# A hybrid decoder layer on one core: first blocks and half the old states loaded before the mixing stage, U built first, two slices of the output weights split inside the second pass

## What is computed

```python
p = h @ w_in                                   # projection, h = rmsnorm(x)
qkv = silu(causal_conv(p[..., :QKV_DIM], ...))
# chunked gated delta rule: T = inverse of a 64x64 unit triangular matrix per head
u = einsum('bnhij,bnjhd->bnhid', T, v_beta)
w = einsum('bnhij,bnjhd->bnhid', T, k_beta * exp(gc)[..., None])
def step(S, inp):
    v_new = u_n - einsum('bhid,bhde->bhie', w_n, S)
    o = einsum('bihd,bhde->bhie', q_n, S) * exp(g_n) + einsum('bhij,bhje->bhie', qk_n, v_new)
    S = S * exp(g_last) + einsum('bihd,bhie->bhde', k_dec, v_new)
# sample rows: one recurrent step on state_delta (8 requests x 4 heads, 128x128 each)
kv = einsum('bhd,bhde->bhe', k_t, S);  delta = (v_t - kv) * b_t
y = concatenate([o_a, o_b]) @ w_o              # o_b is the chunk gMLP
```

## Time and profile before

| | |
|---|---|
| median of 3 runs | 2351.67 us (2350.78 to 2353.48) |
| the profiled execution | 2351.88 us, its span 2350.2 us |
| TensorE busy | 2284.8 us, 97% of the span |
| VectorE, ScalarE, GpSimd busy | 1567.8, 1003.7, 764.7 us |
| mean granted TensorE clock | 0.988 of full |

### The profile page before, as it was taken

How to read it: one execution, slowest core, us unless ns; L and a number is a source line. 1 busy time by engine, 2 the same in 40 slices (tenths; PEclk the granted TensorE clock), 3 DMA queues, 4 the chain that set the end, 5 groups by cost and what they waited for, 6 DMA issues and landing times.

```text
span 2350.2 us, 34043 instructions
## 1 busy us (share of the span) xinstructions
PE 2284.8 (97%) x12644; PEld 2083.6 (89%) x12644; DVE 1567.8 (67%) x2312; ACT 1003.7 (43%) x1969; POOL 764.7 (33%) x654
## 2 busy tenths in 40 slices
PE   7999999999899999989999999999999999999996
PEld 5999999999888888779999999999887878787875
DVE  6535564487676565687657645644777987887788
ACT  5333332211243444266667667766522322232225
POOL 4000001000112121264463643434543443444335
PEclk9999999999889999999999999999999999999998
DMA  5022434322665445538644533464432313231303
GB/s 182 29 82 79 114 89 142 116 99 72 198 186 158 141 136 154 171 121 244 206 149 147 166 127 120 145 201 140 182 139 81 99 45 99 81 99 36 99 28 144
DMA packets 303911, 296.64 MB, mean 126 GB/s; under 512 B 41196, under 2 KB 243152, under 8 KB 300412
## 3 DMA queue, kind: packets, MB, share of 16 engines
q1 hardware_dynamic: 303748, 294.48, 39.8%
HBM read 205.08 MB, written 89.44 MB: 125 GB/s over the span
## 4 chain that ended last, share of the span: by engine, by line
PE 53%; DVE 3%; ACT 1%; issue 1%; DVEq 0%; ACTq 0%
PE bank L120 17%; PE bank L121 17%; PE bank L122 17%; PE bank L2777 1%; DVE f_acc L2660 1%; PE bank L2861 1%; PE bank L2859 1%; DVE f_up_cut L2576 0%; DVE f_h_cut L2580 0%; DVE f_acc L2650 0%; DVE f_z_cut L2630 0%; DVE xn L2611 0%; DVE f_part L2617 0%; ACT f_h_cut L2351 0%; PE bank L2800 0%
## 5 line engine op out<-in xcount | busy, mean ns | idle before, releaser
L120 PE MATMUL bank<-f_h_cut,f_up_cut 128*128 128x344 f32 x1344 | 431.5, 321 | 6.4 <-DVE f_part L2617 3.4
L121 PE MATMUL bank<-f_h_cut,f_up_cut 128*128 128x344 f32 x1344 | 431.2, 321 | 0.0
L122 PE MATMUL bank<-f_h_cut,f_up_cut 128*128 128x344 f32 x1344 | 429.0, 319 | 0.0
L120 PE MATMUL bank<-f_dn_cut,f_z_cut 128*128 128x512 f32 x896 | 351.0, 392 | 5.0 <-ACT f_z L2394 2.8
L121 PE MATMUL bank<-f_dn_cut,f_z_cut 128*128 128x512 f32 x896 | 350.1, 391 | 0.0
L122 PE MATMUL bank<-f_dn_cut,f_z_cut 128*128 128x512 f32 x896 | 350.1, 391 | 0.0
L2650 DVE TENSOR_TENSOR f_acc<-bank,f_acc 128x1024 f32<-128x1024 f32 x224 | 269.8, 1218 | 103.1 <-PE bank L122 102.9
L120 PE MATMUL bank<-h_hi,w_lo 128*128 128x412 f32 (+1 forms) x960 | 336.7, 351 | 0.0
L121 PE MATMUL bank<-h_lo,w_hi 128*128 128x412 f32 (+1 forms) x960 | 335.9, 350 | 0.0
L122 PE MATMUL bank<-h_hi,w_hi 128*128 128x412 f32 (+1 forms) x960 | 335.8, 350 | 0.0
L120 PEld LDWEIGHTS bank<-f_h_cut,f_up_cut 128*128 128x128 f32 x1344 | 252.4, 188 | 10.0 <-DVE f_up_cut L2576 7.7
(11 more groups left out here) (463 smaller groups left out, 4105.1 us busy)
## 6 DMA issues: line engine op xcount, KB each, us to landing
z_dram<-f_z SPq DMA_DIRECT2D x96, 344.0 KB, 2.2
p_dram<-ffn_gains SPq DMA_DIRECT2D x24, 1024.0 KB, 4.6
xn<-z_dram SPq DMA_DIRECT2D x44, 512.0 KB, 3.7
f_dn_raw<-in_w_down_dram SPq DMA_DIRECT2D x32, 512.0 KB, 6.5
up_raw<-in_w_up_dram SPq DMA_DIRECT2D x25, 512.0 KB, 4.1
up_raw<-in_w_in_dram SPq DMA_DIRECT2D x24, 512.0 KB, 5.7
f_up_raw<-in_w_up_dram SPq DMA_DIRECT2D x24, 512.0 KB, 4.4
f_up_raw<-in_w_up_dram SPq DMA_DIRECT2D x40, 256.0 KB, 4.6
```

The lines of the kernel that those rows point to most:

```text
L120: pe.matmul(out, wl, xh, start=start and k == 0, stop=False, skip_group_check=skip)
L121: pe.matmul(out, wh, xl, start=False, stop=False, skip_group_check=skip)
L122: last = pe.matmul(out, wh, xh, start=False, stop=stop and k == n - 1, skip_group_check=skip)
```

## The change

Four things move; no arithmetic is added or left out.

1. In `project`, SyncE stores the second part of the blocks as soon as it is made, waits until it has landed, loads the first chunk's T64 and N21 and the sample states of heads 0 and 1 (two loads of 512 KB), and only then stores the last tile of p. Its closing waits now ask for these loads. In `mix` these loads are gone.
2. VectorE builds U of chunk 0 ahead of `dve_norms`; `dve_rows` takes its old place in pass 0.
3. ScalarE runs `decay` of chunk 0 at the end of pass 0 instead of after its first copy.
4. Slice 0 of the output weights is cut high inside pass 1, and slices 0 and 1 are cut low inside pass 1.

```diff
@@ project, SyncE
+            def load_first_inverse():
+                keys.store_blocks(eng, 1)
+                eng.wait_ge(c.tb_stored, 32)
+                blocks_of = io["t_dram"].rearrange("(b h c) (i j) -> b c i h j", b=2, h=H, j=HALF)
+                at = slice(5 * HW, 5 * HW + H * HALF)
+                for b in range(2):
+                    eng.dma_start(heads(c.xn_room[b * HALF:(b + 1) * HALF, at]), blocks_of[b, 0]).then_inc(inverse_loaded, 16)
+                eng.dma_start(c.xn_room[HALF:P, 6 * HW:6 * HW + H * HALF], io["n21_dram"][0]).then_inc(inverse_loaded, 16)
+                eng.wait_ge(s_conv_made, 1)
+                rooms = c.ab_room[:, 0:NHB // 2 * P].rearrange("p (n v) -> p n v", v=P)
+                for h in range(H // 2):
+                    eng.dma_start(rooms[:, h * NS:(h + 1) * NS, :],
+                                  io["state_delta"][0, :, h].rearrange("b k v -> k b v")).then_inc(states_loaded, 16)
...
+                if t == NT - 1:
+                    load_first_inverse()
...
-            keys.store_blocks(eng, 1)
             eng.wait_ge(first_loaded, 16 * 4)
+            eng.wait_ge(inverse_loaded, 16 * 3)
+            eng.wait_ge(states_loaded, 16 * (H // 2))
@@ dve_pass
             if f == 0:
-                dve.wait_ge(s["zeroed"], 3)
-            build_u(dve, f)
-            if f == 0:
                 rows.dve_rows(dve)
+            else:
+                build_u(dve, f)
...
             ins.then_inc(s["s_updated"], 1)
+            if n == 1:
+                cut_w_o_lo(dve, 0)
...
             dve.tensor_scalar(epsq[f % 2][:], ssq[:], EPS, DK * EPS, ALU.add, ALU.mult).then_inc(s["epsq_made"], 1)
+            if n == 1:
+                cut_w_o_lo(dve, 1)
@@ act_pass
-        if f == 0:
-            decay(act, f)
...
             ins.then_inc(s["o_squared"], 1)
+        if n == 1:
+            cut_w_o_hi(act, 0)
         if F:
...
             act.activation(xs[:], bY[0:HALF, 0:H * HALF], ACT.Copy).then_inc(s["xs_made"], 1)
+        if f == 0:
+            decay(act, f)
@@ mix, VectorE
             dve.memset(ms[:], 1.0).then_inc(s["zeroed"], 1)
+            rows.dve_products(dve)
+            dve.wait_ge(s["t64_loaded0"], 32)
+            dve.wait_ge(s["zeroed"], 3)
+            build_u(dve, 0)
             rows.dve_norms(dve)
...
-                    for k in range(KT):
+                    for k in range(2, KT):
                         cut_w_o_lo(dve, k)
...
-                    for k in range(KT):
+                    for k in range(1, KT):
                         cut_w_o_hi(act, k)
```

More of the change, by code:

```diff
@@ L526, in project @@
     y_stored = c.y_stored
-    first_loaded = sem("first_loaded")
+    first_loaded, inverse_loaded, states_loaded = sem("first_loaded"), sem("inverse_loaded"), sem("first_states_loaded")
     w_in = io["w_in"][0].rearrange("(k p) n -> p k n", p=P)
@@ L943, in load_states @@
     def load_states(self, sp):
[L944 to L949, removed]
+        for h in range(H // 2):
+            sp.sem_inc(self.s["states_loaded"], 16)
+        for h in range(H // 2, H):
+            at = (h % (H // 2)) * NS
+            sp.dma_start(self.states[1][:, at:at + NS, :],
+                         self.io["state_delta"][0, :, h].rearrange("b k v -> k b v")).then_inc(self.s["states_loaded"], 16)
     def store_rows(self, sp):
@@ L1046, in pool_masks, with dve_products @@
         pool.tensor_tensor(heads(self.dmask[u]), across(self.d_rows[:]), along(self_mask), ALU.mult).then_inc(self.s["dmask_made"], 1)
+    def dve_products(self, dve):
+        dve.tensor_tensor(self.prod[:], self.q, self.k, ALU.mult).then_inc(self.s["prod_made"], 1)
     def dve_norms(self, dve):
@@ L1053, in dve_norms @@
         by_row = lambda ap: ap.rearrange("p (h b) -> p h b", h=H)
-        dve.tensor_tensor(self.prod[:], self.q, self.k, ALU.mult).then_inc(s["prod_made"], 1)
         did(dve.tensor_tensor(by_row(self.og[:]), c.s_gate[:], self.og_col.unsqueeze(2).to_broadcast([P, H, NS]), ALU.mult))
@@ L1487, in inverse @@
         def inverse():
-            if f == 0:
-                sp.wait_ge(c.tb_stored, 32)
             wait(sp, s["u_turned"], f - 1)
@@ L1518, in load_raw @@
         if f == 0:
-            for loaded in ("v_loaded", "gate_loaded0", "qt_loaded0", "kt_loaded"):
+            for loaded in ("v_loaded", "gate_loaded0", "qt_loaded0", "kt_loaded", "t64_loaded0", "t64_loaded0", "n21_loaded0"):
                 sp.sem_inc(s[loaded], 16)
-        for part in (decay, gmlp_rows, inverse) if f == 0 else (decay, values, keys_tile, queries, inverse, gmlp_rows) if f == 1 else (inverse, queries, decay, keys_tile, values, gmlp_rows):
+        for part in (decay, gmlp_rows) if f == 0 else (decay, values, keys_tile, queries, inverse, gmlp_rows) if f == 1 else (inverse, queries, decay, keys_tile, values, gmlp_rows):
             part()
```

## The result

The changed kernel takes 2354.51 us (median of 22 runs, 2352.91 to 2356.7); the kernel before took 2351.72 us beside it (22 runs, 2347.52 to 2353.48). The ratio is 1.0014, with a 95% interval of 1.0008 to 1.0020: 2.8 us slower, where 3.8 us faster was forecast, and above the top of the range (2351.6). The profiled execution took 2355.78 us, with a span of 2354.1 us.

What follows compares the result with a forecast made beforehand. TensorE, busy 97% of the span, was taken as the bound, with two chains meeting at 666.46 us. Delta 3.1 us sooner plus 0.7 for the clock gave 3.8 us: median 2347.9 us, 8-in-10 range 2345.3 to 2351.6.

Steps and rivals of the forecast that it cites:

- rival E: Pass 1: slice 0 is not there when ScalarE comes to cut it, at about 642; 2353.9 us, chance 0.05.
- SyncE loses the wait and loads at 623.54 and two state loads (together about 5.6 us): SyncE's queue in the mixing stage: about 5.6 us removed ahead of slice 0, argued against its late landing.
- the table load and first exponential end at 631.6: End of pass 0, ScalarE: the moved decay's first exponential is done at 631.6 us, then GpSimd's product and mask until 633.5.
- All three signs of being wrong: Block ends later than 620, ScalarE waits for slice 0, or full clock comes at another place than taken.
- Block's end: End of the projection: early block and state loads are hidden, and the block ends 0.4 us sooner.
- I take 4: End of the projection: the two state loads land 4 us after the last one's issue, at 617.3 us.
- Rival D: Projection's closing waits hold the block until the states land, all engines start 4.8 us late; 2352.3 us, chance 0.07.
- Pass 0: Mixing stage: no wait for U, about 2 us wait for the mask, R 1.8 us sooner, between 0 and 3.1.
- Pass 1: Mixing stage: cuts inside the pass cost little; the states' products start 1.3 us sooner, at 646.7 us.
- I take 0.5: Pass 1, ScalarE: one high cut ahead of the k copy costs 0.5 us, between 0 and 1.06.
- Weights' chain: Output weights: last load at 653.3 instead of 655.81 us, rows' delta at about 663.3 instead of 666.46, 3.1 us sooner.
- Clock: TensorE, 667 to 670 us: the low clock follows the wait before delta; 1.5 us if gone, 0.7 taken.

Runs made afterwards that it cites:

- the tables back: Changed kernel with the first chunk's two decay exponentials put back ahead of ScalarE's copies of k; 2351.73 us.
- room for g: Changed kernel with g of chunk 1 loaded into a second tile, so its load waits for nothing; cuts and exponentials stay as changed; 2351.88 us.
- the room alone: Kernel before with one edit, a tile of its own for g of chunk 1; 2351.93 us.
- the cuts back: Changed kernel with all sixteen cuts of the output weights behind pass 1 again, exponentials still late; 2351.11 us.
- room and cuts back: Changed kernel with a second tile for g of chunk 1 and all cuts behind pass 1 again; 2351.26 us.

## Why the prediction was wrong, by its own steps

**The step that failed** is the one against rival E: "SyncE loses the wait and loads at 623.54 and two state loads (together about 5.6 us)". It lost them, and its queue reached the load of g for chunk 1 at 623.9 us, 3.8 us sooner than before. But what stands there is `wait(sp, s["eg_made"], f)`, and the exponential that it waits for had been moved to 631.12. I priced the moved piece for GpSimd and TensorE ("the table load and first exponential end at 631.6", measured 631.12) and did not list SyncE among those who wait for it. The chance of 0.05 for rival E rested on this. Its outcome is what came: slice 0 late, ScalarE waiting ahead of the copies of k, 2353.9 us forecast for it, 2354.5 measured. (By its own delta, 668.5 against 666.46, the forecast is 2353.9 for the profiled execution and 2353.7 as a median.) That the size fits is in part luck: slice 0 landed at 644.5, not 647.2, since it was issued 1.7 us sooner and landed in 6.6 us instead of 7.5, and the copies of k came 1.2 us later than before, not 3.9. The 32 first small products, 1.7 us longer, made up for much of it. All three signs of being wrong that the prediction names came: the block ended after 620, ScalarE waited for slice 0, and the full clock came at another place.

**Block's end.** Forecast 0.4 us sooner and hidden. The first profile has TensorE's first product 0.6 us later (620.65 against 620.05), but the other profiles have 620.24 and 618.85 against 620.76, so that single profiles don't tell it. The wait ahead of this product does: 2.79 us in all four profiles with the old end of the projection, 2.31 and 2.29 us in the two with only the blocks loaded early (0.5 us sooner, as forecast), and 2.38 to 3.30 us, 2.81 in the mean, in the eight with the states early too. So the early states took the forecast gain back. What was mis-sized is their landing ("I take 4"): the later of the two took 5.6 us and was there at 619.3, not 617.3. Rival D's mechanism took part, at about 0.5 us instead of 4.8.

**Pass 0.** Right in the profile it was made for. No wait for U; a wait of 1.43 us for the mask (forecast about 2) with GpSimd as releaser; R at 636.41 (636 to 637), 1.97 us sooner (1.8 taken). Over all profiles the gain at R is smaller: it comes 15.8, 17.2 and 15.9 us behind the stage's start, before 18.3 and 16.8, in the mean 1.3 us sooner. The table load of 1.28 us at 629.20 is followed at 630.49 by the exponential. The drain of about 1380 ns that the Trainium skill (ScalarE: Activation LUTs, "What ACT_TABLE_LOAD costs") adds is not seen here either.

**Pass 1.** "I take 0.5" for the high cut in front of the copies of k: measured 2.11 us of waiting and 0.96 us from the cut's start to the copies'. So the copies came at 645.53 against 644.35, and the states' products at 650.11 instead of the forecast 646.7. With the tables back there was no such wait, and the copies came 22.9 us behind the stage's start, against 24.9, 26.2 and 25.8 in the changed kernel (24.3 and 22.8 before).

**Weights' chain.** Last slice forecast at 653.3, measured 656.34: the slices were behind the same pause and the late cuts. Where the pause or the cuts were taken away it went out at 652.05 to 654.31. Delta: forecast 663.3, measured 668.11 (668.66 and 668.19 in the other profiles). TensorE doesn't wait for it any more, and VectorE's part was done at 666.22: the chain that ends last at this place is now TensorE's own, 4.8 us later than its forecast 663.3; the states' products alone began 3.4 us later than forecast, behind the late copies of k, and their first half took 1.7 us more.

**Clock.** "I take 0.7" for the stretch of 667 to 670 us: it is at full clock now (1.00), as hoped. But the low clock came earlier in its place: it is there from 646.5 to 667 us, where the kernel before had it from 650 to 663.5 and from 667 to 670.4, and the first group of small products alone took 1.73 us more than in the earlier trace rows. In the kernel before it fell at 650 us, with TensorE at work without a wait since 647.4, so "0.50 after each wait named above" is true of this trace, but isn't all of it: what sets the clock here stays open.

**The gain that never came.** With the wait removed (room for g, with or without the cuts), the stage is 57.4 to 57.8 us long in the profiles, 1.5 to 1.9 below the mean of the kernel before, and the medians still show nothing (2351.26 to 2351.88 against 2350.6 to 2350.8). The kernel before reaches 58.2 us in its second profile without any edit (and 57.6 with the room alone, which took no wait away), and the part behind the stage moves by up to 2.5 us in one kernel. So the forecast gain of 3.8 us, sure to have been seen in these intervals (about 2 us each side), is refuted even for the repaired change; whether up to 2 us of it are there stays open. One place where it can go is TensorE's clock behind the stage: the four profiles with the earliest update of S in pass 2 (676.67 to 677.55: the cuts back, the room for g, room and cuts back, and the kernel before with the room) all have a low stretch near 965 or 985 us, and need 1671.4 to 1672.4 us from there to the end, against 1669.7 and 1670.1 in the two profiles of the kernel before. No run isolated this.

## What to carry to other kernels

An instruction that is moved later has every engine that waits for its result as a reader, and the DMA queue is one: list all waits on its semaphore, also those that protect the *input* tile from being overwritten, and look what stands behind them in the queue. A load that is taken out of a queue brings the queue sooner to its next wait (3.8 us here); it doesn't bring the loads behind that wait. An operand that a cut needs in the middle of a critical chain must be shown to arrive by the new time. Here three repairs took the loss away, the exponentials put back, the cuts put back and a second tile for the blocking load, and none gained anything that these runs can tell.

## What the runs showed of the hardware

TensorE's granted clock fell to 1.2 GHz for 3.4 or 6.8 us near 967 and 987 us in some executions of the changed kernel and not in others, with the same instructions; near 1005 us it fell in all five profiles of the two kernels, for 3.4 us in four and for 6.8 in one. The time behind the stage was 1672.5, 1671.6 and 1670.0 us with three, two and one of these stretches in the changed kernel. I had not expected so large a spread in a stretch that the change leaves alone: a difference of 1 us between two single profiles of this kernel can't be given to an edit. The low clock also came without a wait: the first 32 small products took 5.26 and 6.56 us in the two profiles of the kernel before, and 6.98 to 6.99 us in the three of the changed one and in the runs with the tables back and with the room for g, whether TensorE had waited 3.33 us or 0.4 us ahead of them.
